# Who compares the token ranks: the one-hot lists of a mixture-of-experts stage made by VectorE instead of GpSimd

## The chip, the cores and the metric

The kernel runs on one core of a Trainium2 chip. The time is the device time of one execution in microseconds (us). The kernel before took 1979.54 us in the median of three runs (1977.51 to 1983.85).

## What is computed

One decoder layer on 512 tokens of width 1024, in float32. Three token mixers (latent attention, sliding-window attention with sinks, cross-attention to 256 memory tokens) are gated and summed, and a mixture of experts follows. The change lies in the mixture alone:

```python
logits = xt @ w_router + b_router                 # 512 x 32
top_vals, top_idx = lax.top_k(logits, 4)          # 4 experts for each token
gates = softmax(top_vals)
# for each expert e, on the rows of the tokens that chose it:
gu  = xb @ w_gate_up[e] + b_gate_up[e]            # 1024 -> 2048
hdn = min(glu, 7) * sigmoid(1.702 * glu) * (clip(lin, -7, 7) + 1)
y   = hdn @ w_down[e] + b_down[e]                 # 1024 -> 1024
# out[token] += gate * y, then an RMS norm of the whole layer
```

## The kernel before

**Stages.** The mixers take the first 580 us or so. Then the router's result is turned into tables, and a loop goes over the 32 experts: 30 of them in a hardware loop of two experts a turn (line 1782 on VectorE, 730 on GpSimd), the last two written out. A loop for experts with more than 128 tokens follows; it runs only if there are any.

**Precision by splitting.** Each float32 weight tile of 128x2048 (12 for each expert) is split in two: ScalarE copies it to `w_hi` (`esplit`, line 890), VectorE subtracts that from the raw tile to get `w_lo` (`esplit`, line 1652), and TensorE multiplies hi by hi, lo by hi and hi by lo. The raw tiles are loaded by SyncE's queue into 8 buffers, each as soon as VectorE has made the `w_lo` of the tile before it in that buffer. So every engine handles every weight, and the order of each engine's work is written out by hand.

**Lists of tokens.** `rank_e[p, t, e]` holds the place of token (t, p) in the list of expert e, or -1. `picks[p, t, j]` is 1 where that rank is j: a one-hot comparison of a row of slot numbers `slots_f` (0 to 127) with one column of `rank_e`, four times (t = 0 to 3), 128x128 elements each. TensorE multiplies `picks` with `val_e` (`pick_sum`, line 1204) and gets one number for each of the 128 places of the list: token and choice in one. `find_rows` on VectorE (line 1638) turns it, in four short instructions that each wait for the one before, into `asg_sb` (where the result row is stored) and `tok_sb` (which token is fetched). GpSimd then fetches the rows of x (`gather`, line 700, an indirect DMA to `xg`), and later stores the 128 result rows (`scatter`, line 709, an indirect DMA from `y_sb` to `y_rows`).

**The lists two experts ahead.** In the kernel before, GpSimd makes `picks` for expert e+2 after it has issued the gather for expert e+1 (`pick_expert`, line 693): it copies the column of `rank_e` to `rank_c`, because the expert's number is in a register there, and makes the four comparisons with `rank_c`. For the first expert VectorE makes them itself (line 1635), and the expert's number is a constant there.

**The order on VectorE in expert n** (`body`, line 1731): `select`; `find_rows` for expert n+1, which waits until the store of expert n-1 has landed (line 1641), since `asg_sb` has only two columns and that store reads one of them; `esplit` of tiles 5 and 6; `swiglu(0)`, whose last instruction writes `h_sb` (line 1717); `esplit` 7 and 8; and so on. TensorE in expert n (line 1269) takes tiles 1 to 4, then tile 5, which needs VectorE's `esplit(5)`, then `turn_hidden(0)` (line 1244), which needs `h_sb`, then tiles 6 and 7, the down projection 8 to 11, with the first tile of expert n+1 between. At the end of expert n ScalarE copies the result to `y_sb` (line 919), and GpSimd's scatter of it begins.

Of the kernel before, what the change touches and what calls it, by code (L numbers as in the profile page):

```python
# [22 lines left out]
P = 128  # L23
ALU = mybir.AluOpType
ACT = mybir.ActivationFunctionType
AX = mybir.AxisListType
F32 = mybir.dt.float32
# [8 lines left out]
T = SEQ // P  # L36
# [10 lines left out]
NE, TOPK, DE = 32, 4, 1024  # L47
# [140 lines left out]
def build_layer(nc, x, mem, positions, g_mix, w_in, g_mla_q, w_mla_uq, g_mla_kv, w_mla_ukv, w_mla_o,  # L188
# [30 lines left out]
    with ExitStack() as ctx:  # L219
# [4 lines left out]
        def at(name, shape, dt, kb, extra=0):  # L224
            size = int(np.prod(shape[1:])) * (2 if dt == BF16 else 4)
            off = int(kb * K) + extra
            assert base + off + size <= nc.sbuf_top, (name, off, size)
            return nc.alloc_sbuf_tensor_at(name, shape, dt, offset=base + off)
# [73 lines left out]
        o = int(206.5 * K)  # L302
# [32 lines left out]
        picks = at("picks", [P, T, P], F32, 168)  # L335
# [5 lines left out]
        slots_f = at("slots_f", [P, P], F32, 198.5)  # L341
        rank_e = at("rank_e", [P, T, NE], F32, 199)
# [22 lines left out]
        rank_o = at("rank_o", [P, T], F32, 203.875)  # L365
        asg_sb = at("asg_sb", [P, 2], U32, 203.9375)
        tok_sb = at("tok_sb", [P, 2], U32, 204)
        idx_t = at("idx_t", [P, 2], F32, 204.0625)
        rank_c = at("rank_c", [P, T], F32, 204.125)
        GT = at("GT", [3 * NE, SEQ], F32R, 132)  # L370


# [10 lines left out]
        def sem(name):  # L383
            return ctx.enter_context(nc.semaphore(name))
# [27 lines left out]
        route_ready, list_ready, gt_ready = sem("route_ready"), sem("list_ready"), sem("gt_ready")  # L412
        xg_clear = sem("xg_clear")
        pick_ready, pick_summed, tok_ready = sem("pick_ready"), sem("pick_summed"), sem("tok_ready")
        shift_ready, rank_copied = sem("shift_ready"), sem("rank_copied")
        xg_in, xt_turned, xt_hi, xt_ready = sem("xg_in"), sem("xt_turned"), sem("xt_hi"), sem("xt_ready")
        gu_done, g_ready, sig_ready, hid_ready = sem("gu_done"), sem("g_ready"), sem("sig_ready"), sem("hid_ready")
        ht_turned, ht_hi, ht_ready = sem("ht_turned"), sem("ht_hi"), sem("ht_ready")
# [1 line left out]
        pool_awake = sem("pool_awake")  # L420
# [42 lines left out]
        def expert_slot(i, par):  # L463

            def slot(w):
                c = par * CH + w
                return c % RAW, i * (2 * CH // RAW) + (c // RAW + 1)
            return slot
# [169 lines left out]
        def _(pool):  # L638
# [11 lines left out]
            for a, n in ((0, 32), (32, 16)):  # L650
                for i in range(n):
                    last = pool.memset(inv_f[:, a + i:a + i + 1], float(np.float32(THETA ** (-i / n))))
# [29 lines left out]
                               base=0, pattern=[[1, NE]], channel_multiplier=-1).then_inc(route_ready, 1)  # L682
            pool.wait_ge(route_ready, 9)

            def pick(ranks, n):

                pool.wait_ge(pick_summed, n)
                pool.sem_inc(pool_awake, 1)
                for t in range(T):
                    last = pool.tensor_scalar(picks[:, t, :], slots_f[:, :], ranks[:, t:t + 1], None, ALU.is_equal)  # L690
                last.then_inc(pick_ready, 1)

            def pick_expert(e, n):
                pool.wait_ge(pick_summed, n)
                pool.tensor_copy(rank_c[:, :], rank_e[:, :, e].rearrange("p t o -> p (t o)")).then_inc(rank_copied, 1)
                pool.wait_ge(rank_copied, n)
                pool.sem_inc(pool_awake, 1)
                pick(rank_c, n)

            def gather(par, n):  # L700

                pool.wait_ge(tok_ready, n + 1)
# [14 lines left out]
            pool.wait_ge(xg_clear, 1)  # L717
            pool.wait_ge(hs_stored, 16 * T)
            gather(0, 0)
            pick_expert(slice(1, 2), 1)  # L720

            def body(e, par, ahead):

                if ahead >= 1:
                    gather((par + 1) % 2, e + 1)
                if ahead >= 2:
                    pick_expert(bass.ds(e + 2, 1), e + 2)
                scatter(par, e)

            with pool.Fori(0, NE // 2 - 1) as i:  # L730
# [7 lines left out]
            with pool.If(n_over > 0):  # L738
                with pool.Fori(0, MAX_OVER) as j:
                    with pool.If(j < n_over):  # L740
                        pool.wait_ge(shift_ready, j + 1)
                        pick(rank_o, j + NE)
                        pool.wait_ge(y_stored, j * 16 + 16 * (NE + 1))
                        gather(0, j + NE)
                        scatter(0, j + NE)
# [595 lines left out]
        def _(dve):  # L1341
            chain = [0]

            def link(ins):

                chain[0] += 1
                ins.then_inc(dve_chain, 1)
                dve.wait_ge(dve_chain, chain[0])
# [62 lines left out]
            for s in steps:  # L1411
# [40 lines left out]
                elif s[0] == "turn":  # L1452
                    kind, n = s[1], ticket_of[s]
# [27 lines left out]
                elif s[0] == "mm":  # L1481
                    _, name, ci, oi = s
                    p = panels[name]
# [3 lines left out]
                    t = p["outs"][oi][0]  # L1487
# [56 lines left out]
                elif s[0] == "S":  # L1544
                    u = s[1]
                    kind, hh, _ = units[u]
                    n, scale = unit_size(units[u])
# [15 lines left out]
                elif s[0] == "gain":  # L1563
                    t = s[1]
# [3 lines left out]
                elif s[0] == "turn_h":  # L1568
                    t = s[1]
# [64 lines left out]
            for t in range(T):  # L1634
                last = dve.tensor_scalar(picks[:, t, :], slots_f[:, :], rank_e[:, t, 0:1], None, ALU.is_equal)
            last.then_inc(pick_ready, 1)

            def find_rows(par, n, blocks_stored):

                dve.wait_ge(pick_summed, n + 1)  # L1640
                dve.wait_ge(y_stored, blocks_stored * 16 + 16)
                p1 = PTb[:, 0:1]
                dve.tensor_scalar(idx_t[:, 0:1], p1, 0.0, NOWHERE, ALU.is_equal, ALU.mult).then_inc(find_chain, 1)  # L1643
                dve.wait_ge(find_chain, n * 3 - 2)
                dve.scalar_tensor_tensor(idx_t[:, 1:2], p1, -1.0, idx_t[:, 0:1], ALU.add, ALU.add).then_inc(find_chain, 1)
                dve.wait_ge(find_chain, n * 3 - 1)
                dve.tensor_copy(asg_sb[:, par:par + 1], idx_t[:, 1:2]).then_inc(find_chain, 1)
                dve.wait_ge(find_chain, n * 3)
                dve.tensor_scalar(tok_sb[:, par:par + 1], asg_sb[:, par:par + 1], 2, None,  # L1649
                                  ALU.logical_shift_right).then_inc(tok_ready, 1)  # L1650

            def esplit(w, n, place):
                slot, rs = w % ERING, place(w)[0]
                dve.wait_ge(hi_ready, n * CH + (NF + w + 1))
                dve.tensor_tensor(lo[slot][:, :], raw_moe[rs][:, :], hi[slot][:, :].bitcast(F32),  # L1655
                                  ALU.subtract).then_inc(lo_ready, 1)
# [4 lines left out]
            link(dve.scalar_tensor_tensor(idx_t[:, 1:2], PTb[:, 0:1], -1.0, idx_t[:, 0:1], ALU.add, ALU.add))  # L1661
            link(dve.tensor_copy(asg_sb[:, 0:1], idx_t[:, 1:2]))
            dve.tensor_scalar(tok_sb[:, 0:1], asg_sb[:, 0:1], 2, None, ALU.logical_shift_right).then_inc(tok_ready, 1)

            dve.wait_ge(gexp_done, 1)
            gsum = mx[:, 0:T]
# [64 lines left out]
            def body(n, par, ahead, place, place_next=None):  # L1731
                select(n)
                if ahead:
                    find_rows(1 - par, n + 1, n)
                esplit(5, n, place)
                esplit(6, n, place)
                swiglu(0, n)
                esplit(7, n, place)
                esplit(8, n, place)
                hidden_lo(0, n)  # L1740
                esplit(9, n, place)
                if ahead:
                    x_lo(1 - par, 0, n + 1)
                esplit(10, n, place)
                swiglu(1, n)
                if ahead:
                    x_lo(1 - par, 1, n + 1)
                esplit(11, n, place)
                hidden_lo(1, n)
                if ahead:  # L1750
                    esplit(12, n, place)
                    esplit(1, n + 1, place_next)
                    esplit(2, n + 1, place_next)
                    esplit(3, n + 1, place_next)
                    esplit(4, n + 1, place_next)
# [25 lines left out]
            esplit(4, 0, expert_slot(0, 0))  # L1781
            with dve.Fori(0, NE // 2 - 1) as i:
                for par in range(2):
                    body(i * 2 + par, par, True, expert_slot(i, par), expert_slot(i, par + 1))
            body(NE - 2, 0, True, expert_slot(NE // 2 - 1, 0), expert_slot(NE // 2 - 1, 1))
            body(NE - 1, 1, False, expert_slot(NE // 2 - 1, 1))
            n_over = dve.value_load(over_n[0:1, 0:1], min_val=0, max_val=MAX_OVER)
            with dve.If(n_over > 0):
                with dve.Fori(0, MAX_OVER) as j:
                    with dve.If(j < n_over):  # L1790
                        e = dve.value_load(over_ei[0:1, bass.ds(j, 1)], min_val=0, max_val=NE - 1)
                        dve.wait_ge(pick_ready, j + NE)
                        dve.tensor_scalar(rank_o[:, :], rank_e[:, :, bass.ds(e, 1)].rearrange("p t o -> p (t o)"),
                                          over_b[:, bass.ds(j, 1)], None, ALU.subtract).then_inc(shift_ready, 1)
                        find_rows(0, j + NE, j + NE)
                        x_lo(0, 0, j + NE)
                        x_lo(0, 1, j + NE)
                        for w in range(5):
                            esplit(w, j + NE, further_slot(j))
                        body(j + NE, 0, False, further_slot(j))  # L1800
# [50 lines left out]
```

## Time and profile before

| | |
|---|---|
| median of three runs | 1979.54 us |
| span of the profiled execution | 1989.7 us |
| TensorE busy (matmul) | 1788.3 us, 90% |
| VectorE busy | 1466.1 us, 74% |
| ScalarE busy | 1103.6 us, 55% |
| GpSimd busy | 270.9 us, 14% |
| mean granted TensorE clock | 0.959 of full speed |
| from `find_rows` of one expert to that of the next | 1284.4 us for 30, from 612.08 to 1896.48 us |

The profile is of one execution, and its span is from the first to the last instruction; there is no record of what lies around it. Busy shares are means over stages with different limits. For each engine the trace also tells what ended its idle time ("released by"), and the chain of waits follows the work that ended last back to its start. In timelines a matmul's end is modelled, so neighbours overlap a little, and VectorE's successive instructions do too.

### The profile page before, as it was taken

How to read it: one execution, taken by the hardware profiler on the slowest of the kernel's cores; microseconds unless marked ns; L12 is line 12 of the kernel's file. 1: busy time of each engine (PE TensorE's matmuls, PEld its weight loads, DVE VectorE, ACT ScalarE, POOL GpSimd, SP SyncE). 2: the span in 40 equal slices, each digit the busy share in tenths (PEclk: the TensorE clock that was granted, in tenths of full speed). 3: DMA queues.
4: the chain of work that ended last, by engine and by line, in shares of the span. 5: the costliest groups of instructions: out<-in, count | busy, mean ns of one | idle time of the engine just before them, and what ended most of it. 6: DMA issues, size and time to landing. Idle time of an engine off the chain costs nothing.

```text
span 1989.7 us, 25573 instructions
## 1 busy us (share of the span) xinstructions
PE 1788.3 (90%) x8260; PEld 1412.2 (71%) x8261; DVE 1466.1 (74%) x1723; ACT 1103.6 (55%) x1168; POOL 270.9 (14%) x293
## 2 busy tenths in 40 slices
PE   6899999999879989999988999998999998999994
PEld 5777777877767777777766777776777776777773
DVE  6755454543469788888778888878888878888888
ACT  5423444332246656566656667656666665757663
POOL 1000000000001122111222111212111212111200
PEclk9999999999979999999999999999999999999997
DMA  6311111124167988888888888988898888898885
GB/s 234 107 43 43 43 43 64 64 85 139 44 217 273 311 291 307 299 314 307 309 306 294 308 313 303 314 316 294 304 319 297 317 313 288 300 322 297 318 299 226
DMA packets 209419, 476.90 MB, mean 240 GB/s; under 512 B 18348, under 2 KB 20652, under 8 KB 209304
## 3 DMA queue, kind: packets, MB, share of 16 engines
q1 hardware_dynamic: 199544, 457.33, 65.8%
q0 software_dynamic: 9248, 16.80, 2.6%
q10 hardware_dynamic: 576, 2.10, 0.3%
q8 instruction: 30, 0.49, 0.1%
q14 instruction: 21, 0.17, 0.0%
HBM read 471.97 MB, written 20.97 MB: 248 GB/s over the span
## 4 chain that ended last, share of the span: by engine, by line
PE 54%; DVE 16%; DMA 15%; issue 10%; ACT 4%; ACTq 0%; DVEq 0%; POOLq 0%; SPq 0%
DMA y_rows<-y_sb,asg_sb 14%; PE SC L1264 11%; PE PA L1232 7%; DVE w_lo L1655 7%; PE PA L985 6%; PE SC L1266 6%; PE PA L987 6%; PE PA L986 6%; PE PA L1234 4%; ACT w_hi L895 2%; PE OB L1145 2%; PE PTb L1218 1%; DVE w_lo L1355 1%; PE OB L1247 1%; DVE g_sb L1709 1%
## 5 line engine op out<-in xcount | busy, mean ns | idle before, releaser
L1655 DVE TENSOR_TENSOR w_lo<-w_raw_moe,w_hi 128x2048 fp32r<-128x2048 f32 x384 | 862.5, 2287 | 44.3 <-ACT w_hi L895 44.1
L895 ACT ACTIVATE w_hi<-w_raw_moe 128x2048 fp32r<-128x2048 f32 x384 | 718.3, 1909 | 35.9 <-PE PA L1234 35.7
L1232 PE MATMUL PA<-w_hi,exT_hi 128*128 128x512 f32 x1024 | 348.9, 423 | 56.6 <-DVE w_lo L1655 54.8
L1232 PE MATMUL PA<-w_lo,exT_hi 128*128 128x512 f32 x1024 | 333.2, 408 | 0.0
L1234 PE MATMUL PA<-w_hi,exT_lo 128*128 128x512 f32 x1024 | 329.5, 404 | 0.0
L1232 PEld LDWEIGHTS PA<-w_hi,exT_hi 128*128 128x128 f32 x1024 | 185.9, 196 | 110.0 <-DVE w_lo L1655 67.4
L906 ACT ACTIVATE s_sb<-g_sb 128x512 f32<-128x512 f32 x64 | 40.5, 633 | 375.2 <-DVE g_sb L1709 375.2
L1234 PEld LDWEIGHTS PA<-w_hi,exT_lo 128*128 128x128 f32 x1024 | 202.1, 197 | 47.1
L1232 PEld LDWEIGHTS PA<-w_lo,exT_hi 128*128 128x128 f32 x1024 | 201.3, 197 | 46.7
L712 POOL DMA_INDIRECT y_rows<-y_sb,asg_sb x32 | 64.4, 2011 | 811.5 <-ACT y_sb L923 811.5
L1264 PE MATMUL SC<-w_hi,hT_hi 128*128 128x512 f32 x512 | 160.8, 395 | 1.5 <-DVE hT_lo L1722 1.5
L1264 PE MATMUL SC<-w_lo,hT_hi 128*128 128x512 f32 x512 | 158.0, 390 | 0.0
L1266 PE MATMUL SC<-w_hi,hT_lo 128*128 128x512 f32 x512 | 158.0, 390 | 0.0
L1643 DVE TENSOR_SCALAR idx_t<-PTb 128x1 f32<-128x1 f32 x31 | 4.9, 158 | 178.9 <-DMA y_rows<-y_sb,asg_sb 178.9
L985 PE MATMUL PA<-w_hi,xT_hi 128*128 128x512 f32 (+2 forms) x320 | 129.6, 405 | 1.2 <-DVE attT_lo L1477 1.2
L1355 DVE TENSOR_TENSOR w_lo<-w_raw,w_hi 128x1024 fp32r<-128x1024 f32 (+5 forms) x67 | 81.7, 1232 | 57.1 <-ACT w_hi L758 56.6
L987 PE MATMUL PA<-w_hi,xT_lo 128*128 128x512 f32 (+2 forms) x320 | 122.1, 381 | 0.0
L986 PE MATMUL PA<-w_lo,xT_hi 128*128 128x512 f32 (+2 forms) x320 | 121.7, 380 | 0.0
L705 POOL DMA_INDIRECT xg<-xn_rows,tok_sb x32 | 69.6, 2176 | 367.9 <-DVE tok_sb L1649 293.8
L1266 PEld LDWEIGHTS SC<-w_hi,hT_lo 128*128 128x128 f32 x512 | 96.1, 188 | 20.4
L1264 PEld LDWEIGHTS SC<-w_lo,hT_hi 128*128 128x128 f32 x512 | 96.1, 188 | 20.4
L1264 PEld LDWEIGHTS SC<-w_hi,hT_hi 128*128 128x128 f32 x512 | 93.7, 188 | 19.7 <-DVE hT_lo L1722 1.7
(304 smaller groups left out, 2326.5 us busy)
## 6 DMA issues: line engine op xcount, KB each, us to landing
w_raw_moe<-in_w_gate_up SPq DMA_DIRECT2D x512, 512.0 KB, 6.4
w_raw_moe<-in_w_down SPq DMA_DIRECT2D x128, 1024.0 KB
w_raw<-in_w_in SPq DMA_DIRECT2D x17, 1024.0 KB, 5.0
yk_early<-y_rows SPq DMA_DIRECT2D x12, 512.0 KB, 8.8
w_raw<-in_w_mem_kv SPq DMA_DIRECT2D x4, 1024.0 KB, 7.9
w_raw<-in_w_out SPq DMA_DIRECT2D x4, 1024.0 KB, 9.8
rows<-in_x SPq DMA_DIRECT2D x4, 512.0 KB, 12.1
w_raw<-in_w_mla_o SPq DMA_DIRECT2D x2, 1024.0 KB, 5.1
```

What stands on the lines that cost most here:

```text
L705: pool.indirect_dma_start(xg[:, :], None, xn_rows, bass.IndirectOffsetOnAxis(ap=tok_sb[:, par:par + 1], axis=0), bounds_check=SEQ - 1, oob ...
L712: pool.indirect_dma_start(y_rows, bass.IndirectOffsetOnAxis(ap=asg_sb[:, par:par + 1], axis=0), y_sb[:, :], None, bounds_check=SEQ * TOPK ...
L895: act.activation(hi[slot][:, :], raw_moe[rs][:, :], ACT.Copy).then_inc(hi_ready, 1)
L985: pe.matmul(ps, parts[0], w_hi, start=first, stop=False)
L986: pe.matmul(ps, parts[0], w_lo, start=False, stop=False)
L987: return pe.matmul(ps, parts[1], w_hi, start=False, stop=last)
L1232: pe.matmul(PA[2 * half + s_][:, :], x_h, part[slot][:, w[s_]], start=first, stop=False)
L1234: last = pe.matmul(PA[2 * half + s_][:, :], x_l, hi[slot][:, w[s_]], start=False, stop=False)
L1264: pe.matmul(SC[s_][:, :], hT_hi[:, k, :], part[slot][:, w[s_]], start=first, stop=False)
L1266: last = pe.matmul(SC[s_][:, :], hT_lo[:, k, :], hi[slot][:, w[s_]], start=False, stop=(k == KT - 1))
L1355: ins = dve.tensor_tensor(lo[c % RING][:, a:b], raw[:, c % RING, a:b], hi[c % RING][:, a:b].bitcast(F32), ALU.subtract)
L1655: dve.tensor_tensor(lo[slot][:, :], raw_moe[rs][:, :], hi[slot][:, :].bitcast(F32), ALU.subtract).then_inc(lo_ready, 1)
```

## The change

The comparisons for experts 1 to 31 are made by VectorE (`pick_next`), directly after the `find_rows` of the expert before, and read the column of `rank_e` in place as the scalar operand. GpSimd keeps the gathers and scatters alone; `rank_c` and its semaphore go. `body` on VectorE gets `ahead` as a number, 2 in the loop, 1 and 0 in the last two experts, so that `pick_next` is issued 30 times there and once before the loop. In the loop for experts with more than 128 tokens the comparisons move too.

```diff
@@ GpSimd
-            def pick(ranks, n):
-                pool.wait_ge(pick_summed, n)
-                pool.sem_inc(pool_awake, 1)
-                for t in range(T):
-                    last = pool.tensor_scalar(picks[:, t, :], slots_f[:, :], ranks[:, t:t + 1], None, ALU.is_equal)
-                last.then_inc(pick_ready, 1)
-
-            def pick_expert(e, n):
-                pool.wait_ge(pick_summed, n)
-                pool.tensor_copy(rank_c[:, :], rank_e[:, :, e].rearrange("p t o -> p (t o)")).then_inc(rank_copied, 1)
-                pool.wait_ge(rank_copied, n)
-                pool.sem_inc(pool_awake, 1)
-                pick(rank_c, n)
...
             gather(0, 0)
-            pick_expert(slice(1, 2), 1)
...
                 if ahead >= 1:
                     gather((par + 1) % 2, e + 1)
-                if ahead >= 2:
-                    pick_expert(bass.ds(e + 2, 1), e + 2)
                 scatter(par, e)
@@ VectorE
+            def pick_next(e, n):
+                dve.wait_ge(pick_summed, n)
+                for t in range(T):
+                    last = dve.tensor_scalar(picks[:, t, :], slots_f[:, :], rank_e[:, t, e], None, ALU.is_equal)
+                last.then_inc(pick_ready, 1)
...
             dve.tensor_scalar(tok_sb[:, 0:1], asg_sb[:, 0:1], 2, None, ALU.logical_shift_right).then_inc(tok_ready, 1)
+            pick_next(slice(1, 2), 1)
...
                 if ahead:
                     find_rows(1 - par, n + 1, n)
+                if ahead > 1:
+                    pick_next(bass.ds(n + 2, 1), n + 2)
                 esplit(5, n, place)
                 esplit(6, n, place)
                 swiglu(0, n)
```

## Rows read from the trace of the kernel before

**Rows 1.** The page, chain that ended last, shares of the span by line.

```profile
DMA y_rows<-y_sb,asg_sb 14%; PE SC L1264 11%; PE PA L1232 7%; DVE w_lo L1655 7%; PE PA L985 6%; PE SC L1266 6%; PE PA L987 6%; PE PA L986 6%; PE PA L1234 4%; ACT w_hi L895 2%; PE OB L1145 2%; PE PTb L1218 1%; DVE w_lo L1355 1%; PE OB L1247 1%; DVE g_sb L1709 1%
```

**Rows 2.** Waits over the whole span: us in total, times, longest us.

```profile
DVE idx_t L1643 <- DMA y_rows<-y_sb,asg_sb: 178.9, 30, 6.4
...
PE PA L1232 <- DVE w_lo L1655: 54.8, 30, 2.2
...
PE OB L1247 <- DVE h_sb L1717: 45.4, 30, 2.0
```

**Rows 3.** The chain in order of time, one expert: start us, us, what.

```profile
1246.07 9.40 DMA y_rows<-y_sb,asg_sb
```

**Rows 4.** Timeline of VectorE, the same expert: start us, us, instruction.

```profile
1255.49 0.16 DVE L1643 TENSOR_SCALAR idx_t<-PTb 128x1 f32<-128x1 f32 x1 [5.97 <-DMA y_rows<-y_sb,asg_sb]
...
1256.17 4.50 DVE L1655 TENSOR_TENSOR w_lo<-w_raw_moe,w_hi 128x2048 fp32r<-128x2048 f32 x2
...
1262.62 0.74 DVE L1717 TENSOR_TENSOR h_sb<-u_sb,s_sb 128x512 f32<-128x512 f32 x1
```

**Rows 5.** Timeline of TensorE, the same expert.

```profile
1258.51 0.73 PE L1232 MATMUL PA<-w_hi,exT_hi 128*128 128x512 f32 x2 [1.83 <-DVE w_lo L1655]
...
1263.42 0.66 PE L1247 MATMUL OB<-ident,h_sb 128*128 128x128 f32 x4 [1.89 <-DVE h_sb L1717]
```

**Rows 6.** Timeline of VectorE before the loop: its own four comparisons and the next.

```profile
582.82 0.87 DVE L1635 TENSOR_SCALAR picks<-slots_f,rank_e 128x128 f32<-128x128 f32 x4
583.61 2.28 DVE L1655 TENSOR_TENSOR w_lo<-w_raw_moe,w_hi 128x2048 fp32r<-128x2048 f32 x1
```

**Rows 7.** The tile picks: durations ns min/median/max, first and last start us, forms.

```profile
L690 POOL TENSOR_SCALAR picks<-slots_f,rank_c x124: 592/617/951, 589.3 to 1861.1; 128x128 f32<-128x128 f32 x124
L1635 DVE TENSOR_SCALAR picks<-slots_f,rank_e x4: 279/279/288, 582.8 to 583.4; 128x128 f32<-128x128 f32 x4
```

**Rows 8.** Line 1728, an operand addressed by register 30 times and by constant twice.

```profile
L1728 DVE TENSOR_SCALAR sel<-ecol,rowid x32: 268/273/276, 611.9 to 1932.8; 64x128 fp32r x30, 64x128 fp32r<-64x128 f32 x2
L1728 DVEq FUSED_REGOPS  x30: 46/46/52, 608.9 to 1845.3; - x30
```

**Rows 9.** Timeline of VectorE, next-to-last expert, no comparisons on GpSimd.

```profile
1896.48 0.16 DVE L1643 TENSOR_SCALAR idx_t<-PTb 128x1 f32<-128x1 f32 x1 [5.83 <-DMA y_rows<-y_sb,asg_sb]
...
1897.13 4.49 DVE L1655 TENSOR_TENSOR w_lo<-w_raw_moe,w_hi 128x2048 fp32r<-128x2048 f32 x2
...
1903.57 0.69 DVE L1717 TENSOR_TENSOR h_sb<-u_sb,s_sb 128x512 f32<-128x512 f32 x1
```

**Rows 10.** Timeline of GpSimd: the copy before the loop, and in it.

```profile
588.81 0.20 POOL L695 COPY rank_c<-rank_e 128x4 f32<-128x4 f32 x1
...
1259.35 1.36 POOL L695 COPY rank_c<-rank_e 128x4 f32 x1
```

**Rows 11.** Windows: length, busy us (instructions) by engine, then PEclk, DMA share, GB/s.

```profile
1172.90:1176.30 3.40, 3.40 (x9) 2.63 (x9) 3.37 (x4) 0.91 (x2) 3.09 (x5) 0.50 0.58 137
1220.70:1224.10 3.40, 3.40 (x11) 2.72 (x10) 3.40 (x2) 3.40 (x3) 0.09 (x1) 0.50 0.94 355
```

**Rows 12.** Timelines of TensorE and ScalarE, two experts: first `h_sb` transpose, first result copy.

```profile
1177.52 0.66 PE L1247 MATMUL OB<-ident,h_sb 128*128 128x128 f32 x4 [0.30 <-DVE h_sb L1717]
...
1200.71 0.60 ACT L922 ACTIVATE y_sb<-SC 128x512 f32<-128x512 f32 x1 [0.48 <-PE SC L1266]
...
1220.37 0.87 PE L1247 MATMUL OB<-ident,h_sb 128*128 128x128 f32 x4 [1.98 <-DVE h_sb L1717]
...
1244.09 0.60 ACT L922 ACTIVATE y_sb<-SC 128x512 f32<-128x512 f32 x1 [0.49 <-PE SC L1266]
```

**Rows 13.** The tile y_rows: the scatters, and from issue to landing.

```profile
L712 POOL DMA_INDIRECT y_rows<-y_sb,asg_sb x32: 1700/2022/2042, 646.0 to 1963.9; - x32
...
DMA to landing us min/median/max: 3.9/9.3/10.0
```

**Rows 14.** Timeline before the loop: TensorE waits for the first fetched rows.

```profile
595.00 1.12 PE L1218 MATMUL PTb<-ident,xg 128*128 128x128 f32 x4 [0.21 <-DMA xg<-xn_rows,tok_sb]
```

More of the change, by code:

```diff
@@ L368, in build_layer @@
         idx_t = at("idx_t", [P, 2], F32, 204.0625)
-        rank_c = at("rank_c", [P, T], F32, 204.125)
         GT = at("GT", [3 * NE, SEQ], F32R, 132)
@@ L414, in build_layer @@
         pick_ready, pick_summed, tok_ready = sem("pick_ready"), sem("pick_summed"), sem("tok_ready")
-        shift_ready, rank_copied = sem("shift_ready"), sem("rank_copied")
+        shift_ready = sem("shift_ready")
         xg_in, xt_turned, xt_hi, xt_ready = sem("xg_in"), sem("xt_turned"), sem("xt_hi"), sem("xt_ready")
@@ L740, in _ @@
                     with pool.If(j < n_over):
-                        pool.wait_ge(shift_ready, j + 1)
-                        pick(rank_o, j + NE)
                         pool.wait_ge(y_stored, j * 16 + 16 * (NE + 1))
@@ L1783, in _ @@
                 for par in range(2):
-                    body(i * 2 + par, par, True, expert_slot(i, par), expert_slot(i, par + 1))
-            body(NE - 2, 0, True, expert_slot(NE // 2 - 1, 0), expert_slot(NE // 2 - 1, 1))
-            body(NE - 1, 1, False, expert_slot(NE // 2 - 1, 1))
+                    body(i * 2 + par, par, 2, expert_slot(i, par), expert_slot(i, par + 1))
+            body(NE - 2, 0, 1, expert_slot(NE // 2 - 1, 0), expert_slot(NE // 2 - 1, 1))
+            body(NE - 1, 1, 0, expert_slot(NE // 2 - 1, 1))
             n_over = dve.value_load(over_n[0:1, 0:1], min_val=0, max_val=MAX_OVER)
@@ L1791, in _ @@
                         e = dve.value_load(over_ei[0:1, bass.ds(j, 1)], min_val=0, max_val=NE - 1)
-                        dve.wait_ge(pick_ready, j + NE)
+                        dve.wait_ge(pick_summed, j + NE)
                         dve.tensor_scalar(rank_o[:, :], rank_e[:, :, bass.ds(e, 1)].rearrange("p t o -> p (t o)"),
                                           over_b[:, bass.ds(j, 1)], None, ALU.subtract).then_inc(shift_ready, 1)
+                        dve.wait_ge(shift_ready, j + 1)
+                        for t in range(T):
+                            last = dve.tensor_scalar(picks[:, t, :], slots_f[:, :], rank_o[:, t:t + 1], None, ALU.is_equal)
+                        last.then_inc(pick_ready, 1)
                         find_rows(0, j + NE, j + NE)
```

## The prediction, on record before the result was known

> **What bounds the kernel now.** TensorE is 90% busy by the page, and VectorE 74%; by that alone, half a microsecond more on VectorE would be free. So I read the chain of waits first. The largest single item on it in the expert loop is no computation: the store of the result rows, 14% of the span [rows 1]. The table of waits says who is held by it: VectorE's `find_rows` waited for that store 30 times, 178.9 us in all, about 6 us for each expert [rows 2]. The same table shows TensorE idle twice in each expert: 30 times for `w_lo` (54.8 us, 1.8 each) and 30 times for `h_sb` (45.4 us, 1.5 each).
>
> The timelines join these. In the expert at 1255 us the store is issued at 1246.07 and takes 9.40 us [rows 3]. VectorE's `idx_t` starts at 1255.49, after 5.97 us of waiting, and the `w_lo` behind it at 1256.17 [rows 4]. TensorE, which has run out of split tiles, restarts at 1258.51 on that `w_lo`, works three microseconds, and idles 1.89 us more until `h_sb` is there; it restarts at 1263.42, 0.06 us after `h_sb` ends at 1263.36 [rows 4, 5]. From there to the copies of the result it is TensorE's work, then the copies, the store, and `find_rows` again. That is a closed loop: store of expert n-1, `find_rows`, two `w_lo`, `swiglu(0)`, TensorE, store of expert n. Its length is the expert's period, 1284.4/30 = 42.8 us by the table of before. The reader should see that the stretch between `idx_t` and `h_sb` (7.87 us, 1255.49 to 1263.36) lies wholly on the loop: VectorE has just been idle, and TensorE is waiting at the other end. Whatever is put between the two is paid in full in each of the experts.
>
> **The change, part by part.**
>
> *Four comparisons on VectorE, after `find_rows`, before `esplit(5)`.* They stand in exactly that stretch. The trace has the same instruction before the loop: four comparisons of 128x128 from 582.82, and the `w_lo` behind them starts at 583.61, so four of them move what follows by 0.79 us (0.20 each; one alone reads 279 ns, since neighbours overlap) [rows 6, 7].
>
> *Their address by register.* The known case has a constant column. In the loop the column is a register. Line 1728 has one operand addressed by register in 30 cases and by constant in 2, and all 32 lie between 268 and 276 ns, so the engine itself is no slower; the sequencer needs one register instruction of 46 ns for it [rows 8]. Between `idx_t` and `w_lo` the looped code takes 0.68 us and the written-out code, with its constant wait counts, 0.65 [rows 4, 9], so register work there is mostly hidden. The one wait of `pick_next` (`pick_summed`) is satisfied already: `find_rows` has just passed the same count. Three of the four address computations can run under the comparison before (46 ns against 0.20 us); the first, with the wait's count, can't. I take 0.06 us. Sum: 0.85 us an expert. From above, with nothing overlapped, it would be 4 x 0.279 + 5 x 0.046 = 1.35 us.
>
> *The copy and four comparisons leave GpSimd.* GpSimd was never late with them, so their 4 us an expert return nothing directly. What they can return is contention. With them, `h_sb` takes 0.74 us; in the next-to-last expert, where GpSimd has no comparisons, 0.69 [rows 4, 9]. I take that 0.05 as the gain. The whole stretch from `idx_t` to the end of `h_sb` is 7.87 us with and 7.78 without (1896.48 to 1904.26), which bounds the gain at 0.09.
>
> The Trainium skill, SBUF — State Buffer, "Who interferes with whom", says that a VectorE instruction with two SBUF inputs and a GpSimd instruction that reads SBUF exclude each other for a whole instruction. In one direction this trace agrees: GpSimd's copy takes 0.20 us before the loop and 1.36 in it, ending at 1260.71, as VectorE's second `w_lo` does at 1260.67 [rows 4, 10]. In the other direction it doesn't: by the rule each of the last two instructions of `swiglu` could be held for a comparison of some 0.6 us, and taking GpSimd out would then give back up to 1.2 us an expert, more than the change costs; the rows show 0.05 to 0.09.
>
> *The sum for the loop:* 30 experts x (0.85 - 0.05) = 24.0 us.
>
> *Before the loop.* One `pick_next` with constants, 0.79 us of VectorE's time, ahead of the tables that TensorE waits for. TensorE meets the fetched rows at 595.00 after 0.21 us of idleness [rows 14], so some of the delay goes under that wait: 0.5 us. Sum: 24.5 us.
>
> *TensorE's clock.* After an idle stretch the granted clock falls to half (1.2 GHz) for a while: at 1172.9 while tile 5 is multiplied, at 1220.7 after `h_sb` [rows 11]. Where it falls decides its price. In the first case TensorE merely finishes tile 5 later and idles 0.30 us instead of 1.89 to 1.98; from there to the result copy is 23.19 us. In the second the same way takes 23.72 us [rows 12]. So a fall after `h_sb` costs 0.53 us, one before it nothing. By the same two views for the 29 experts from 655 to 1854 us (of which these two stand for their kind), 15 have the dear fall, 8 the free one, 6 none. The change lengthens the first idleness from 1.83 us to about 2.65. Falls should then come more often in the first place, and each one there shortens the second idleness and forestalls the dear one. At best 15 x 0.53 = 8 us return; if on the other hand all 30 experts had the dear kind, 8 us would be added. I can't tell the place in each expert, and take 0.
>
> *Total:* the profiled execution would go from 1989.7 to 2014.2 us. The profile lies 10.2 us above the median of the runs and has nothing recorded around its span; I put the same 24.5 us on the median: 2004.0 us.
>
> **The rivals.**
>
> *Register addressing is dear on VectorE* (chance 0.07). For it: the looped copy of GpSimd, addressed by register, reads 1.36 us against 0.20 by constant [rows 10], and `rank_c` looks like a way to pay that once and not four times. If each comparison paid that 1.16 us, 30 x 4 x 1.16 = 139 us would come, 2144 us; with one payment an expert 35 us more, 2039. Against it: the copy's end coincides with `w_lo`'s, and line 1728 shows no such price [rows 8].
>
> *The delay is absorbed* (0.05): TensorE's 90% is the true bound and the added microsecond is eaten by idleness elsewhere. It would take slack between `idx_t` and `h_sb`, or a later wait that now ends last for another reason. Then only the step before the loop is left, 1980 us. Against it: both restarts of TensorE follow VectorE within 0.1 us [rows 4, 5].
>
> *Faster through the store* (0.03). The store takes from 3.9 to 10.0 us, 9.3 in the median [rows 13]; it shares the DMA engines with the weight loads, which VectorE's `w_lo` release, and GpSimd writes what the DMA reads. If the later loads left it more room or a relieved GpSimd issued it sooner, each expert would gain what the store loses. The point of decision is 0.80 us: at 8.5 us the change costs nothing, at 8.0 us it gives 30 x 0.5 = 15 us, 1964 us. Against it: the store waits for ScalarE's copies of the result, long after GpSimd's comparisons in the order of the code, and everything from `h_sb` to the next `idx_t` keeps its order and its distances.
>
> *The change does only half of what it says*: comparisons of experts beyond 128 tokens move too, but only 32 scatters were issued [rows 13], so that loop never ran and costs nothing either way.
>
> **The numbers.** The forecast (0.85) is 2004.0 us. Its own bounds: per expert 0.79 - 0.09 = 0.70 us gives 21, less 8 from the clock, 1992.5; 1.35 us gives 40.5, 2020, and 8 from the clock 2028. Neither end is near what the rows of the loop show, so for 8 in 10 I take 1994 to 2016. What this kernel's runs can tell from no change is 0.3%, 6 us. Slower by more: 0.92 (forecast 0.85 and the dear register 0.07); within it: 0.05; faster: 0.03.
>
> **What would show it.** In the profile after: four comparisons of about 279 ns on VectorE between `tok_sb` and `w_lo`, the `w_lo` starting about 1.5 us after `idx_t` in place of 0.68; `h_sb` back at 0.69 us; TensorE's wait for `w_lo` up from 54.8 us to about 79, that for `h_sb` the same or less; the wait for the store still about 6 us an expert; the period 43.6 us. A wait for the store that shrank by the length of the comparisons, with the same period, would refute the closed loop; comparisons spaced wider than 0.25 us would put the register price wrong; a changed store time would put the balance elsewhere.

## The result: slower by 2%, outside the forecast range

The changed kernel takes 2018.95 us in the median of four runs (2014.49 to 2026.94), before 1980.71 us. The ratio is 1.0196, 95% interval 1.0172 to 1.0221. In a later set of runs (a0 below) it is 1.0181 (1.0159 to 1.0204). I had forecast 2004.0 us, at most 2016: the direction was right, the size 24.5 us against 36 to 38.

The page after, chain that ended last, shares of the span by line (span 2017.3 us):

```profile
DMA xg<-xn_rows,tok_sb 14%; DMA y_rows<-y_sb,asg_sb 14%; PE SC L1243 11%; PE PA L1211 6%; PE PA L964 6%; PE SC L1245 6%; PE PA L966 6%; PE PA L965 6%; DVE w_lo L1640 3%; PE PA L1213 3%; PE PTb L1197 2%; PE OB L1124 2%; DVE w_lo L1334 1%; PE PTb L1110 1%; PE PA L1220 1%
```

Beside the store, still 14%, there now stands an item that was not on this list in [rows 1]: the gather, the fetch of the x rows, with another 14%. The table of waits after (us in total, times, longest):

```profile
DVE idx_t L1628 <- DMA y_rows<-y_sb,asg_sb: 172.5, 30, 6.5
...
PE PA L1211 <- DVE w_lo L1640: 71.5, 30, 3.1
...
PE PTb L1197 <- DMA xg<-xn_rows,tok_sb: 31.8, 27, 2.1
PE OB L1226 <- DVE h_sb L1703: 31.7, 29, 1.9
```

Against [rows 2], the wait for `w_lo` grew from 54.8 to 71.5 us, that for `h_sb` shrank from 45.4 to 31.7, and TensorE waits 27 times for fetched rows, where it hardly ever did. One expert on VectorE (start us, us):

```profile
1269.64 0.16 DVE L1628 TENSOR_SCALAR idx_t<-PTb 128x1 f32<-128x1 f32 x1 [6.03 <-DMA y_rows<-y_sb,asg_sb]
...
1270.33 0.88 DVE L1620 TENSOR_SCALAR picks<-slots_f,rank_e 128x128 f32<-128x128 f32 x4
1271.12 4.49 DVE L1640 TENSOR_TENSOR w_lo<-w_raw_moe,w_hi 128x2048 fp32r<-128x2048 f32 x2
...
1277.56 0.69 DVE L1703 TENSOR_TENSOR h_sb<-u_sb,s_sb 128x512 f32<-128x512 f32 x1
```

This is close to the forecast: the comparisons shift the `w_lo` by 0.79 us (forecast 0.85), it starts 1.48 us after `idx_t` in place of 0.68 [rows 4], and `h_sb` is back at 0.69. The same expert on TensorE:

```profile
1273.45 0.73 PE L1211 MATMUL PA<-w_hi,exT_hi 128*128 128x512 f32 x2 [2.68 <-DVE w_lo L1640]
...
1278.31 0.66 PE L1226 MATMUL OB<-ident,h_sb 128*128 128x128 f32 x4 [0.58 <-DVE h_sb L1703]
...
1283.47 0.66 PE L1197 MATMUL PTb<-ident,xg 128*128 128x128 f32 x4 [1.78 <-DMA xg<-xn_rows,tok_sb]
```

The first two rows answer [rows 5]; the third is new. The tile xg says why (durations in ns, min/median/max; then from issue to landing):

```profile
L689 POOL DMA_INDIRECT xg<-xn_rows,tok_sb x32: 1091/5194/5203, 590.6 to 1926.0; - x32
...
DMA to landing us min/median/max: 7.0/11.7/12.5
```

GpSimd spends 5.2 us in the gather's instruction. Before, this row read 1100/2208/2254 and landing 6.2/7.0/7.7. GpSimd has less to do than before and its one remaining instruction there takes 3 us longer; the rows land 4.7 us later, behind TensorE's need.

### The profile page after: what moved, and what is told of

It is laid out like the page before. It is cut to its first block, busy times and chain, and to the rows that moved or that the text cites. A ratio compares the mean times of both kernels' runs of the same rounds, so it can differ in the third digit from the quotient of the medians.

```text
span 2017.3 us, 25570 instructions
## 1 busy us (share of the span) xinstructions
PE 1792.2 (89%) x8260; PEld 1410.5 (70%) x8261; DVE 1489.6 (74%) x1847; ACT 1104.5 (55%) x1168; POOL 229.4 (11%) x138
## 4 chain that ended last, share of the span: by engine, by line
PE 52%; DMA 29%; DVE 10%; issue 5%; ACT 3%; POOLq 0%; ACTq 0%; DVEq 0%; SPq 0%
DMA xg<-xn_rows,tok_sb 14%; DMA y_rows<-y_sb,asg_sb 14%; PE SC L1243 11%; PE PA L1211 6%; PE PA L964 6%; PE SC L1245 6%; PE PA L966 6%; PE PA L965 6%; DVE w_lo L1640 3%; PE PA L1213 3%; PE PTb L1197 2%; PE OB L1124 2%; DVE w_lo L1334 1%; PE PTb L1110 1%; PE PA L1220 1%
## 5 line engine op out<-in xcount | busy, mean ns | idle before, releaser
L1211 PE MATMUL PA<-w_hi,exT_hi 128*128 128x512 f32 x1024 | 349.9, 424 | 73.3 <-DVE w_lo L1640 71.5
L689 POOL DMA_INDIRECT xg<-xn_rows,tok_sb x32 | 159.1, 4973 | 367.5 <-DVE tok_sb L1634 293.3
```

The source lines that it names most:

```text
L689: pool.indirect_dma_start(xg[:, :], None, xn_rows, bass.IndirectOffsetOnAxis(ap=tok_sb[:, par:par + 1], axis=0), bounds_check=SEQ - 1, oob ...
L1211: pe.matmul(PA[2 * half + s_][:, :], x_h, part[slot][:, w[s_]], start=first, stop=False)
```

## The experiments

All keep the work of the expert loop. Unused comparisons, reductions or subtractions write to tiles that nothing reads. "Gather" is the duration of the instruction on GpSimd; in the 30 experts of the loop it always starts 1.65 to 1.68 us after `idx_t`. The ratio is to runs of the kernel before made at the same time (medians 1985.36 us for the first four rows, 1990.59 for e_reduce, e_bfill, e_gap and e_ts2, 1992.21 for the rest). Where it says "one run" there is a single timed run and no interval.

| run | first `w_lo` after `idx_t`, us | gather, us (median) | ratio to before |
|---|---|---|---|
| b0: before | 0.68 | 2.21 | 0.9999 (0.9986 to 1.0012) |
| a0: changed | 1.48 | 5.20 | 1.0181 (1.0159 to 1.0204) |
| e_idle | 0.68 | 2.20 | 0.9973 (0.9959 to 0.9986) |
| e_between | 0.68 | 2.20 | 1.0129 (1.0108 to 1.0151) |
| e_reduce | 1.42 | 2.93, 5 times 5.13 | 1.0096 (1.0077 to 1.0115) |
| e_bfill | 1.43 | 5.15 | 1.0171 (1.0153 to 1.0189) |
| e_gap | 1.48 | 3.00 | 1.018, one run |
| e_ts2 | 1.03 | 2.55, 4 times 4.75 | 1.004, one run |
| e_idle2 | 0.68 | 2.20 | 0.9984 (0.9973 to 0.9995) |
| e_both | 0.68 | 2.21 | 1.0008 (0.9995 to 1.0020) |
| e_third | 1.48 | 5.60 | 1.022, one run |
| e_ts3 | 1.23 | 4.94 | 1.011, one run |

### b0 and a0: both kernels, unchanged, on one chip

> The kernel before, unchanged, profiled on the chip that also runs the three others, because the first profile of before (1989.7 us) lay above all its timed runs. Both theories: ratio 1.00, the gather (fetch of x rows) takes 2.2 us on GpSimd, 42.8 us an expert, and a span nearer to 1980 us than to 1990.

> The changed kernel, unchanged. Ratio 1.015 to 1.022 again, gather 5.2 us in 30 experts, TensorE waits for the fetched rows about 1 us in most experts, 43.5 us an expert.

Line `idx_t` of each (durations; first and last start us), b0 first:

```profile
L1643 DVE TENSOR_SCALAR idx_t<-PTb x31: 140/158/160, 615.1 to 1891.7; 128x1 f32<-128x1 f32 x31
```

```profile
L1628 DVE TENSOR_SCALAR idx_t<-PTb x31: 139/158/160, 616.7 to 1933.2; 128x1 f32<-128x1 f32 x31
```

Thirty experts take 1276.6 us before and 1316.5 after, 42.55 and 43.88 each: 39.9 of the 41.3 us between the spans (1984.9 and 2026.2) come from the loop. By the timelines of both, in means over the 30: from `idx_t` to TensorE's restart on `h_sb` 8.00 and 8.76 us (+0.76); from there to the result copy 23.35 and 23.81 (+0.45); from the store's issue to the next `idx_t` 9.23 and 9.35 (+0.12, which differs as much between two profiles of the same kernel: 9.42 in the first profile of before). Between the copy and the store's issue lie 1.97 us in both. The first is my sum; the second is what I left out.

### e_idle: the comparisons in VectorE's idle time

```diff
                 select(n)
-                if ahead:
-                    find_rows(1 - par, n + 1, n)
                 if ahead > 1:
                     pick_next(bass.ds(n + 2, 1), n + 2)
+                if ahead:
+                    find_rows(1 - par, n + 1, n)
```

> The changed kernel with the four comparisons moved in front of find_rows, into the 6 us in which VectorE waits for the store. My theory (the delay between idx_t and h_sb is paid in full, and it makes the gather late): both go, gather 2.2 us, h_sb takes 0.69 us, ratio 0.999 (1.5 us better than before by the lost contention). Rival (leaving GpSimd idle, not the delay, makes the gather slow): gather stays 5.2 us and 0.3 us an expert remain, ratio 1.005.

Timeline of VectorE and then of GpSimd:

```profile
1033.95 0.86 DVE L1620 TENSOR_SCALAR picks<-slots_f,rank_e 128x128 f32<-128x128 f32 x4
1039.85 0.16 DVE L1628 TENSOR_SCALAR idx_t<-PTb 128x1 f32<-128x1 f32 x1 [5.04 <-DMA y_rows<-y_sb,asg_sb]
...
1040.54 4.49 DVE L1640 TENSOR_TENSOR w_lo<-w_raw_moe,w_hi 128x2048 fp32r<-128x2048 f32 x2
...
1041.51 2.21 POOL L689 DMA_INDIRECT xg<-xn_rows,tok_sb  x1 [9.00 <-DVE tok_sb L1634]
```

The same instructions, 0.8 us of VectorE's time, now cost nothing: the wait for the store is shorter by as much. The gather is back at 2.2 us with GpSimd just as idle, so the rival falls. This version is 2% faster than the changed kernel, and 0.3% faster than the kernel before.

### e_between: the comparisons behind the first w_lo

```diff
                     find_rows(1 - par, n + 1, n)
+                esplit(5, n, place)
                 if ahead > 1:
                     pick_next(bass.ds(n + 2, 1), n + 2)
-                esplit(5, n, place)
                 esplit(6, n, place)
```

> The changed kernel with the comparisons between esplit(5) and esplit(6). Theory (the gather is held by the w_lo instructions, and what counts is that the first of them starts late): the first w_lo starts 0.68 us after idx_t again, so the gather takes 2.2 us again; h_sb is still 0.8 us late, ratio 1.012 (24 us) and no wait of TensorE for the fetched rows. Rival (the comparisons themselves hold up the gather, which is issued 1.66 us after idx_t): here they run from 2.9 to 3.7 us after idx_t, while the gather still works, and it takes 3 us or more.

```profile
1050.65 0.16 DVE L1628 TENSOR_SCALAR idx_t<-PTb 128x1 f32<-128x1 f32 x1 [5.84 <-DMA y_rows<-y_sb,asg_sb]
...
1051.33 2.29 DVE L1640 TENSOR_TENSOR w_lo<-w_raw_moe,w_hi 128x2048 fp32r<-128x2048 f32 x1
1053.54 1.00 DVE L1620 TENSOR_SCALAR picks<-slots_f,rank_e 128x128 f32<-128x128 f32 x4
1054.32 2.29 DVE L1640 TENSOR_TENSOR w_lo<-w_raw_moe,w_hi 128x2048 fp32r<-128x2048 f32 x1
...
1052.31 2.20 POOL L689 DMA_INDIRECT xg<-xn_rows,tok_sb  x1 [9.02 <-DVE tok_sb L1634]
```

`h_sb` is as late as in the changed kernel (restart 8.73 us after `idx_t`), but the gather is not touched. This run has the delay without the slow gather: 1.0129, that is 25.6 us on 1985.4. The changed kernel takes 10 us more (1.0181 less 1.0129, 0.0052 x 1985). The two differ in the slow gather, but also in where TensorE's clock falls; with that taken into account (step by step, below) the gather's share is nearer 17 us than 10.

### e_reduce: another kind of instruction in the place

The comparisons as in e_idle, and `filler()` behind `find_rows`:

```diff
+                for t in range(4):
+                    dve.tensor_reduce(dummy[t][:, 0:1], slots_f[:, :], AX.X, ALU.max)
```

> The comparisons in the idle time before find_rows, and in their old place four reductions of slots_f (128x128 to 128x1, results unused): about the same 0.8 us on VectorE, but another kind of instruction, with one input. Theory (only the time at which the first w_lo starts counts): gather 5.2 us, TensorE waits for the fetched rows, ratio 1.018 as the changed kernel. Rival (the comparisons as such, one-input two-output-port instructions or their register operand, hold up the gather): gather 2.2 us, ratio 1.012 by the 0.8 us alone.

Two experts on GpSimd, and the line in all:

```profile
968.98 2.93 POOL L690 DMA_INDIRECT xg<-xn_rows,tok_sb  x1 [9.68 <-DVE tok_sb L1639]
...
1011.84 5.14 POOL L690 DMA_INDIRECT xg<-xn_rows,tok_sb  x1 [8.73 <-DVE tok_sb L1639]
...
L690 POOL DMA_INDIRECT xg<-xn_rows,tok_sb x32: 1094/2928/5137, 591.5 to 1918.6; - x32
```

Neither expectation held. The gather takes 2.93 us in 25 experts, which is the end of the first `w_lo` plus 0.9, and 5.13 in five, the end of the second plus 0.9. There are two outcomes and nothing between: in both groups the first `w_lo` starts 1.40 to 1.42 us and the gather 1.65 to 1.68 us after `idx_t`.

### e_bfill: the kernel before, delayed

```diff
                 if ahead:
                     find_rows(1 - par, n + 1, n)
+                    for t in range(4):
+                        dve.tensor_scalar(dummy[t][:, :], slots_f[:, :], rank_e[:, t, 0:1], None, ALU.is_equal)
                 esplit(5, n, place)
```

> The kernel before, GpSimd still making its copy and comparisons, with four unused comparisons on VectorE after find_rows. Theory: the delay alone makes the gather slow, 5.2 us, and GpSimd's own comparisons now come 3 us later; ratio 1.018 to 1.020. Rival (GpSimd, relieved of its work, takes longer over the gather, for instance because what followed in its queue hurried it): gather 2.2 us, ratio 1.012.

```profile
L706 POOL DMA_INDIRECT xg<-xn_rows,tok_sb x32: 1096/5149/5210, 591.2 to 1928.1; - x32
...
L691 POOL TENSOR_SCALAR picks<-slots_f,rank_c x124: 590/776/4834, 592.9 to 1896.3; 128x128 f32<-128x128 f32 x124
```

GpSimd still does all its work, and the gather is slow all the same. What makes it slow is what VectorE does, not what GpSimd no longer does. The time of the changed kernel is reproduced (1.0171) with nothing moved.

The second line shows that the hold-up is not special to a DMA. GpSimd's comparisons now come later and meet VectorE's next pair of `w_lo`. In each of the 30 experts the third comparison starts 0.05 to 0.15 us after that pair begins, and takes 4.73 to 4.83 us in place of 0.6: it ends 0.4 us after the pair does, and was not let in between the two.

### e_gap and e_third: a gap in the run of w_lo, and a longer run

Both are the changed kernel. e_gap has two reductions between the two `w_lo`, e_third two subtractions of 128x128, both inputs in SBUF, behind them:

```diff
                 esplit(5, n, place)
+                    for t in range(2):          # e_gap
+                        dve.tensor_reduce(dummy[t][:, 0:1], slots_f[:, :], AX.X, ALU.max)
                 esplit(6, n, place)
+                    for t in range(2):          # e_third
+                        dve.tensor_tensor(dummy[t][:, :], slots_f[:, :], ident[:, :], ALU.subtract)
```

> The changed kernel with two unused reductions (0.4 us, one input, so not the kind of w_lo) between the first and the second w_lo. Theory (the gather is locked out by each w_lo, and the second follows the first too closely to let it in): it gets in when the first w_lo ends, 3.77 us after idx_t, and ends 0.9 us later, so 3.0 us in place of 5.2. Rival (the gather is slow for a length of its own, whatever VectorE runs): 5.2 us still, or 5.6 with the second w_lo's end.

> The changed kernel with two unused two-input subtractions (0.4 us, both inputs in SBUF) directly behind the second w_lo. Theory A (the gather, once inside a run of two-input instructions without a gap, waits for the end of the run): gather ends 0.9 us after the last of them, 5.6 us. Theory B (it is passed over once only, by the second w_lo): 5.2 us as before. The delay of 0.4 us is on the path as well, 12 us more than the changed kernel.

e_gap, VectorE, then GpSimd:

```profile
1012.46 2.29 DVE L1641 TENSOR_TENSOR w_lo<-w_raw_moe,w_hi 128x2048 fp32r<-128x2048 f32 x1
1014.66 0.47 DVE L1727 TENSOR_REDUCE dummy<-slots_f 128x1 f32<-128x128 f32 x2
1015.05 2.28 DVE L1641 TENSOR_TENSOR w_lo<-w_raw_moe,w_hi 128x2048 fp32r<-128x2048 f32 x1
...
1012.63 3.00 POOL L690 DMA_INDIRECT xg<-xn_rows,tok_sb  x1 [9.04 <-DVE tok_sb L1635]
```

e_third, VectorE, then GpSimd:

```profile
1237.16 4.48 DVE L1641 TENSOR_TENSOR w_lo<-w_raw_moe,w_hi 128x2048 fp32r<-128x2048 f32 x2
1241.57 0.48 DVE L1728 TENSOR_TENSOR dummy<-slots_f,ident 128x128 f32<-128x128 f32 x2
...
1237.35 5.60 POOL L690 DMA_INDIRECT xg<-xn_rows,tok_sb  x1 [9.00 <-DVE tok_sb L1635]
```

In e_gap the first `w_lo` ends at 1014.75 and the gather at 1015.63, 0.88 us later; the second `w_lo` doesn't hold it. In e_third the last subtraction ends at 1242.05 and the gather at 1242.95, 0.90 later. In the changed kernel the second `w_lo` ends at 1275.61 and the gather (issued at 1271.29, 5.20 us) at 1276.49, again 0.88. So a gather that was not let in at the end of the first `w_lo` stays out for as long as VectorE runs two-input instructions without a gap, and finishes 0.9 us after the gap begins. Both results agree with theory A to 0.02 us; B falls. They are clean, for the first `w_lo` begins at 1.48 us in both as in the changed kernel, and all 30 experts of each do the same. It is only for a run that begins early (0.68 us) that the end of the first `w_lo` is enough, without any gap. Whether the reductions let it in because they have one input, or because they write one column, was not tested.

### e_ts2 and e_ts3: how late is too late

As e_reduce, with two and three unused comparisons in the place.

> Comparisons before find_rows, and two unused ones (0.4 us) in their old place, so the first w_lo starts 1.08 us after idx_t in place of 0.68 or 1.48. Theory (the gather asks for the first time at one fixed moment, and is stopped once if a w_lo runs already, twice if not): the gather takes either 2.6 us (first w_lo's end at 3.37 plus 0.9, from 1.66) or 4.8 us (second w_lo's end at 5.57 plus 0.9), nothing between, and the same in all experts. Rival (gradual sharing): about 3.7 us, halfway between 2.2 and 5.2.

> Comparisons before find_rows, and three unused ones in their old place, so that the first w_lo starts about 1.23 us after idx_t. Theory (one fixed moment; e_ts2 at 1.03 was on the near side, e_bfill at 1.42 to 1.44 on the far side, e_reduce at 1.41 to 1.42 on both): 1.23 is on the near side, gather 2.75 us in all experts (1.23 + 2.29 + 0.89 - 1.66), no wait of TensorE for fetched rows. Rival (the moment lies anywhere between): 5.0 us.

```profile
L690 POOL DMA_INDIRECT xg<-xn_rows,tok_sb x32: 1093/2547/4753, 588.5 to 1905.6; - x32
```

```profile
L690 POOL DMA_INDIRECT xg<-xn_rows,tok_sb x32: 1092/4944/4952, 590.7 to 1920.2; - x32
```

With the first `w_lo` at 1.03 us the gather is fast in 26 of 30 experts (2.55) and slow in four (4.75); at 1.23 slow in all. My expectation for e_ts3 was wrong, and so was one fixed moment: behind comparisons the edge lies at 1.03 to 1.23 us, behind reductions 1.42 is still mostly on the fast side. What remains is that the outcome has two values, and that behind comparisons a later start of the run makes the slow one likelier (none of 30 at 0.68 us, 4 at 1.03, all at 1.23 and later).

### e_idle2 and e_both: is the lead of e_idle real, and whose is it

> The version with the comparisons before find_rows once more, beside the next kernel, on another occasion. Expected ratio 0.997 again if its lead over before is real, 0.999 to 1.000 if only the 0.06 us by which its stretch from idx_t to h_sb is shorter (30 x 0.06 = 2 us) counts.

> The kernel before with its copy and comparisons on GpSimd, and four unused comparisons on VectorE in the idle time before find_rows. Theory (comparisons in the idle time are free, and the lead of the version before comes from GpSimd's work being gone): ratio 1.000, gather 2.2 us, h_sb 0.74 us. Rival (the lead comes from something else in the place, such as the shorter idleness of VectorE): 0.997.

The lead is real but small: 0.9973 and, on another occasion, 0.9984, both intervals below 1. With GpSimd's comparisons kept and VectorE's unused ones added in the same idle time, 1.0008: nothing. So the comparisons in that place are free, and the lead of 3 to 5 us goes with GpSimd's missing work, though the intervals of e_idle2 and e_both touch at 0.9995. The shorter way from `idx_t` to the restart (7.94 against 8.00 us in the timelines) explains 2 us of it; the rest I could not place.

## Why the prediction was wrong, step by step

- **The closed loop, and where to read it: right.** Store, `find_rows`, `w_lo`, `swiglu(0)`, TensorE, store. VectorE is 74% busy, and 0.8 us on it lengthened the way from `idx_t` to TensorE's restart by 0.76 us (b0 to a0); six microseconds earlier in the same queue they cost nothing (e_idle).
- **The price of four comparisons with a register address: right, and a little high.** 0.79 us of shift in the loop as before it; the 0.06 us added for register work did not show. The line of all 124 in the trace after:

```profile
L1620 DVE TENSOR_SCALAR picks<-slots_f,rank_e x124: 276/281/289, 589.3 to 1879.7; 128x128 f32<-128x128 f32 x124
```

  The dear-register rival falls (139 us on 2004 would have been 2143, not 2144); the copy's 1.36 us on GpSimd [rows 10] was a lock-out too, and reads 0.20 us in e_bfill, where it comes after the run.
- **The loop's sum of 24.0 us: right in size for what it covers, and closer than it deserves.** e_between measures 25.6 us, but some 4 of these are dear clock falls that the sum took as 0 (below). The delay alone is 30 x 0.73 = 22 us there and 30 x 0.76 = 23 in a0.
- **No term for the gather, and "everything from `h_sb` to the next `idx_t` keeps its order and its distances": the step that failed.** I wrote the quoted words against the rival "faster through the store", and the whole sum takes them for granted. I looked at contention in one direction and for one pair, GpSimd's comparisons against `swiglu`. I did not follow the other instruction of GpSimd in the same stretch, the gather, although VectorE's `tok_sb` releases it just there and the change delays two `w_lo` instructions that run beside it. It was never asked what the delay does to the gather, so it stood in the sum at nothing. The gather grew by 3.0 us, its landing by 4.7, and TensorE waited 36.4 us for it in a0. The way from `h_sb` to the result copy grew by less, 0.45 x 30 = 13.6 us, since TensorE's wait for `exT_lo` (16.7 us in b0) went under it and dear clock falls became fewer. Timed, the changed kernel lies 10 us above e_between, which has no slow gather; but a0 got 3 us back from the clock and e_between lost 4, so the gather's own price is nearer 17 us. Experts with the same kind of fall say the same: from restart to result copy they took 23.15 us in b0 and 23.88 in a0 with a free fall, 23.07 and 23.61 with none, but 23.69 and 23.73 with a dear one, where the slower TensorE reaches the rows no sooner than they land. The first profile of after shows less, so 10 to 17 us is as close as I can put it.
- **The clock: taken as 0, and the expected direction was right.** Free falls, before `h_sb`, rose from 5 to 19 experts and dear ones fell from 13 to 7 (b0 to a0): 6 x 0.53 = 3 us returned. In e_between, where the long idleness lies directly ahead of TensorE's restart on `h_sb` (2.6 to 2.7 us), 21 are dear: 8 x 0.53 = 4 us lost.
- **Before the loop: +0.5 us.** b0 and a0 differ by 1.6 us at the first `idx_t` (615.1 and 616.7), but two profiles of the same kernel, the first of before and b0, differ there by 3.0 (612.1 and 615.1), so this was not tested.
- **The level, and a sign that came true by luck.** The first profile of before (1989.7 us) lay 10 us above its runs; b0 gives 1984.9 with runs of 1985.5. Taking the difference and not the level kept that out of the sum. But the forecast period of 43.6 us started from that profile's 42.8. The first profile of after does read 43.62 us an expert, and the spans of the two are only 27.6 us apart, which looks like the forecast come true; the timed runs are 38 us apart, and b0 and a0 read 42.55 and 43.88. Two single profiles are too few to tell 24 us from 38.

The Trainium skill, SBUF — State Buffer, "Who interferes with whom", which I weighed for GpSimd's reads, also says that a VectorE `tensor_tensor` does not stall the making of a DMA's descriptors on GpSimd; it marks the reason as inferred. Taken for the gather, that would have put its loss at 0. The runs don't bear that out: `w_lo` is a `tensor_tensor`, and the indirect DMA's instruction grows from 1.1 us (the one before the loop, with no `w_lo` beside it) to 2.2, 3.0, 5.2 and 5.6 us, each ending 0.9 us past the end of a `w_lo` or of the run. The rule that the prediction did cite, on GpSimd instructions that read SBUF, would have had the gather held if it counts as one for its list of rows, `tok_sb`; the trace does not show which of its steps is held. Nor is the lock-out mutual here: the `w_lo` pair that the gather runs beside takes 4.48 to 4.50 us wherever the two stand together (once 4.64, in the first profile of before), whether the gather lasts 2.2 or 5.6 us.

**Open.** Why the gather gets in at the border between the two `w_lo` when the run began early (0.68 us), and not when it began late, is not settled; nor why comparisons and reductions ahead of the run move the edge differently, nor why the landing moved by 1.7 us more than the instruction's end. The trace shows no step inside the gather's instruction, and it was not tried to issue the gather at another distance.

## What to carry to other kernels

Cost a moved instruction twice: by its length on the path, and by what its shift does to instructions of other engines released at the same moment, above all to indirect DMAs issued by GpSimd, which a run of two-input VectorE instructions can hold up for its whole length. Before putting work behind a long wait, put it in front: here the same four instructions cost 1.8% behind it and nothing ahead. Where such a DMA must be issued beside VectorE's stream, a short one-input instruction in the stream can let it in, as the two reductions of e_gap did; there they cost as much as they gave back (1.018 in one run).

## What the runs showed that I had not expected

- A gather's instruction on GpSimd lasts 2.2, 2.55, 2.9, 3.0, 4.75, 4.9, 5.2 or 5.6 us by the place of VectorE's subtractions, each the same within 0.07 us in all experts, with two values in one kernel at the edge (e_reduce: 2.93 and 5.13; e_ts2: 2.55 and 4.75).
- Its landing moves by more than its end: from 7.0 to 11.7 us after issue, 4.7 us, while the instruction grows by 3.0.
- A plain comparison on GpSimd that meets a pair of `w_lo` is held for the whole pair as well (e_bfill: 4.8 us in place of 0.6).
- Unused work of 0.4 us in the stream (e_gap) shortened the gather by 2.2 us and took TensorE's wait for it away, but stood on the path itself.
